# A transformer block pair on one core: own lane orders for PE, VectorE and ScalarE in the attention stage, gate rows by transposes, z products in column strips

## What is computed

```python
def first_block(x, c, ...):
    mod = (silu(c) @ w_ada + b_ada)
    h = rms_norm(x, g_pre_mix) * (1 + sc_m) + sh_m
    proj = h @ w_in                      # 2544 columns
    # group a: 8 heads, compressed + selected + window keys, gated sum
    # group b: 8 heads over a latent; an indexer keeps the 64 best of 256 keys per query:
    score = einsum('bths,bth->bts', relu(logits), wi_b)
    _, idx = top_k(score, 64)            # s // 4
    y = concat([o_a, o_b]) @ w_out
    x = x + ga_m * rms_norm(y, g_post_mix)
    x = x + ga_f * rms_norm(swiglu(...), g_post_ffn)

def second_block(x, c, ctx, ...):        # one layer, last: only the context's states are needed
    gq, gk, gv, gz, gg, rq, rk, rv, rg = split(h @ w_in)
    pre = gz.reshape(B, T, 2, 16) @ gla_gate_w + gla_gate_b    # gz is the "z" of the change
    ...
    x = x + mod[2] * x_out
    x = x + mod[5] * expert_choice_ffn(h2, ...)
    return rmsnorm(x, final_norm_w)
```

## Time and profile before

| what | value |
|---|---|
| time of the runs, median | 1354.22 us (1354.01 to 1354.99, 3 runs) |
| span of the profiled execution, first to last instruction | 1351.0 us |
| what the runs have beyond that span | 3.2 us (no other time is given for the profiled execution) |
| busy: PE, PEld, DVE, ACT, POOL | 1004.6, 582.0, 523.5, 292.5, 29.0 us |
| mean granted clock of PE | 0.869 |
| read from HBM | 413.26 MB, 307 GB/s over the span |

### The profile page before, as it was taken

One profiled execution on the slowest core, in us unless ns is written; L12 is line 12 of the kernel. 1 busy time (PEld: TensorE's weight loads), 2 busy tenths in 40 slices (PEclk: granted clock), 3 DMA queues, 4 the chain that ended last, 5 costly groups with the idle time before them and its releaser, 6 DMA issues.

```text
span 1351.0 us, 13067 instructions
## 1 busy us (share of the span) xinstructions
PE 1004.6 (74%) x5454; PEld 582.0 (43%) x5454; DVE 523.5 (39%) x995; ACT 292.5 (22%) x467; POOL 29.0 (2%) x38
## 2 busy tenths in 40 slices
PE   0796888899989999899997766555465555566585
PEld 0585667777666787687873211111111111111131
DVE  6876577687544498578663100000000000000001
ACT  2322344452242333562341100000000000000000
POOL 0001000000000000100110000000000000000000
PEclk9797798899989999899997867788867778766888
DMA  9796221567634469233269999999999999999996
GB/s 387 319 382 246 96 76 63 193 257 277 249 122 158 156 232 357 94 125 125 94 270 431 427 430 430 432 429 430 431 432 429 432 427 433 430 431 431 428 432 270
DMA packets 41147, 415.16 MB, mean 307 GB/s; under 512 B 4928, under 2 KB 4928, under 8 KB 7808
## 3 DMA queue, kind: packets, MB, share of 16 engines
q1 hardware_dynamic: 38304, 405.75, 73.2%
q10 hardware_dynamic: 2784, 8.57, 1.8%
HBM read 413.26 MB, written 1.05 MB: 307 GB/s over the span
## 4 chain that ended last, share of the span: by engine, by line
PE 43%; DMA 42%; DVE 10%; ACT 3%; issue 1%; POOL 0%; DVEq 0%; SPq 0%
DMA ring<-in_w_egu 25%; DMA ring<-in_w_ed 13%; PE PS L658 8%; PE PS L660 8%; PE PS L659 8%; PE PS L959 4%; PE PS L1275 3%; DMA arena<-in_w_ed 2%; PE PS L567 2%; DVE ringR L1496 2%; DMA ring<-in_w_in 1%; PE PS L1337 1%; DVE arena L1368 1%; ACT ringR L2403 1%; DVE ring L1410 1%
## 5 line engine op out<-in xcount | busy, mean ns | idle before, releaser
L1275 PE MATMUL PS<-ring,arena 128*32 128x512 f32 (+1 forms) x1152 | 173.1, 736 | 108.5 <-DMA ring<-in_w_egu 108.4
L658 PE MATMUL PS<-ringR,arenaR 128*128 128x512 f32 (+1 forms) x520 | 213.5, 411 | 21.5 <-DVE arenaR L1479 19.9
L660 PE MATMUL PS<-ringR,arenaR 128*128 128x512 f32 (+1 forms) x520 | 206.8, 398 | 0.0
L659 PE MATMUL PS<-ringR,arenaR 128*128 128x512 f32 (+1 forms) x520 | 206.6, 397 | 0.0
L1496 DVE TENSOR_TENSOR ringR<-ring,ringR 128x2048 fp32r<-128x2048 f32 (+1 forms) x66 | 148.7, 2254 | 98.1 <-ACT ringR L2403 98.0
L1368 DVE SCALAR_TENSOR_TENSOR arena<-arena,PS 128x256 f32<-128x256 f32 (+2 forms) x68 | 33.2, 497 | 370.5 <-ACT arena L2840 363.3
L2403 ACT ACTIVATE ringR<-ring 128x2048 fp32r<-128x2048 f32 (+1 forms) x66 | 123.9, 1885 | 89.2 <-PE PS L660 56.7
L1275 PEld LDWEIGHTS PS<-ring,arena 128*32 128x32 f32 x1152 | 36.3, 129 | 236.1 <-DMA ring<-in_w_egu 174.9
L1337 PE MATMUL PS<-ring,arena 128*32 128x512 f32 x512 | 88.3, 826 | 55.5 <-DMA ring<-in_w_ed 54.9
L658 PEld LDWEIGHTS PS<-ringR,arenaR 128*128 128x128 f32 x520 | 99.1, 191 | 48.1 <-DVE arenaR L1479 20.5
L2840 ACT ACTIVATE arena<-PS 128x512 f32<-128x512 f32 (+1 forms) x12 | 6.7, 561 | 502.6 <-PE PS L1275 502.6
(11 more groups left out here) (343 smaller groups left out, 878.1 us busy)
## 6 DMA issues: line engine op xcount, KB each, us to landing
ring<-in_w_egu SPq DMA_DIRECT2D x48, 2048.0 KB, 35.7
ring<-in_w_ed SPq DMA_DIRECT2D x32, 2048.0 KB, 33.8
ring<-in_w_vad SPq DMA_DIRECT2D x40, 1024.0 KB, 6.9
ring<-in_w_egu SPq DMA_DIRECT2D x24, 1536.0 KB, 29.6
arena<-in_w_egu SPq DMA_DIRECT2D x16, 2048.0 KB, 35.5
ring<-in_w_in SPq DMA_DIRECT2D x22, 1024.0 KB, 4.9
ring<-in_w_gu SPq DMA_DIRECT2D x22, 1024.0 KB, 4.8
arena<-in_w_ed SPq DMA_DIRECT2D x11, 2048.0 KB, 32.4
```

The costliest lines, as they stand in the source:

```text
L658: mm(o, xh(k, t), hi[:, c], start=k == 0, stop=False)
L659: mm(o, xh(k, t), s.viewr[:, c], start=False, stop=False)
L660: i = mm(o, xl(k, t), hi[:, c], start=False, stop=k == nk - 1)
L1275: i = mm(PS[32 * ee:32 * ee + 32, b + a_, 0:fw], XEv[:, k, grp, 32 * ee:32 * ee + 32], wv[:, ee, a_, :], start=k == 0, stop=k == 7, tile_p ...
```

## The change

Three orders of the lanes stand in the place of `ATT`: `ATT_PE` (102 letters), `ATT_DVE` (107) and `ATT_ACT` (93). Steps that do nothing at the end of a lane are left out. `sync` still makes its list of loads from `ATT`, so loads are issued in the same order as before. `gate_rows` uses the transpose helper `tr` instead of a matmul with the identity. The z products go into four strips of 32 output partitions, matmul k into strip k mod 4, two matmuls deep in each; the sum over the strips is left to the gate product, whose weights (`gate_w`) are stored four times, so it now contracts over 128 rows instead of 32, DVE copies 128 partitions instead of 32, and the load of `gate_w` is 256 KB instead of 64 KB.

```diff
 ATT, FFN = schedules()
+ATT_PE = ("p p f f p i c 1 i i 0 f c f 1 0 d d c 0 1 f d f c 1 i i 0 i i f c d 1 c f f c 1 0 f 1 d i i i i i i 0 f c c 1 d c i i 0 1 c f 1 0 f 0 d 0 1 f 1 f c c 0 1 c 0 i i 0 1 f i i 1 o o o 0 1 0 o o 0 o o 1 0 1 0").split()
+ATT_DVE = ("p p p f f c 1 0 d f f i c d c 1 1 0 0 f f d i i i c 1 c 0 f f c d i i o 1 1 c f f 1 d c 0 0 c i i i d c 0 1 1 f f c i 1 0 0 d i i 0 f f c 1 1 c i i 1 c 0 0 i i 0 f f i i 1 1 o o 0 0 i i i i i i 1 0 o o o o 1 1 0 0").split()
...
@@ gate_rows
-                    i = mm(PS[:, bank + c // 4, 128 * (c % 4):128 * (c % 4) + 128], gcol[:, 8 * q + c:8 * q + c + 1].broadcast_to([128, 128]), ident, start=True, stop=True)
+                    i = tr(PS[:, bank + c // 4, 128 * (c % 4):128 * (c % 4) + 128], gcol[:, 8 * q + c:8 * q + c + 1].broadcast_to([128, 128]))
@@ tensor
-            for k in ATT:
+            for k in ATT_PE:
                 next(lanes[k])
@@ context (and the same in w_in2 with bank 6, hT2)
                 for k in range(8):
-                    i = mm(PS[0:32, 7, 0:256], GZW[:, k, :], hcv[:, k, :], start=k == 0, stop=k == 7)
+                    j = k % 4
+                    i = mm(PS[32 * j:32 * j + 32, 7, 0:256], GZW[:, k, :], hcv[:, k, :], start=k < 4, stop=k >= 4, tile_position=(0, 32 * j))
...
-                    mm(PS[:, 7 - t, :], GZc[0:32, 128 * t:128 * t + 128], GWc[0:32, :], start=True, stop=True).then_inc(*sig("pe ctx pre", t))
+                    mm(PS[:, 7 - t, :], GZc[:, 128 * t:128 * t + 128], GWc, start=True, stop=True).then_inc(*sig("pe ctx pre", t))
...
-    d["gate_w"] = gw
+    d["gate_w"] = np.tile(gw, (4, 1))
```

More of the change, by code:

```diff
@@ L87 @@
 ATT, FFN = schedules()
+ATT_PE = ("p p f f p i c 1 i i 0 f c f 1 0 d d c 0 1 f d f c 1 i i 0 i i f c d 1 c f f c 1 0 f 1 d i i i i i i 0 f c c 1 d c i i 0 1 c f 1 0 f 0 d 0 1 f 1 f c c 0 1 c 0 i i 0 1 f i i 1 o o o 0 1 0 o o 0 o o 1 0 1 0").split()
+ATT_DVE = ("p p p f f c 1 0 d f f i c d c 1 1 0 0 f f d i i i c 1 c 0 f f c d i i o 1 1 c f f 1 d c 0 0 c i i i d c 0 1 1 f f c i 1 0 0 d i i 0 f f c 1 1 c i i 1 c 0 0 i i 0 f f i i 1 1 o o 0 0 i i i i i i 1 0 o o o o 1 1 0 0").split()
+ATT_ACT = ("p p f p i f f 1 0 1 c c 0 d d f f i i c c i i 1 1 f f o 1 0 0 f f o 0 c c c i i 1 1 f f 1 i i i i i i 0 0 c c c c 0 f f 1 1 d d d d d 1 0 0 f f 0 i i 1 1 i i 1 0 0 o o 0 i i 1 1 0 0 1 0").split()
 MIX_PE = ("w g w g w g w g g w g g w r g w g w w g g r w g r w g r w g g r w r g g g r w r r r").split()
@@ L1052, in w_in2 @@
                         for k in range(8):
-                            i = mm(PS[0:32, 6, 0:256], GZW[:, k, :], hT2[:, 256 * k:256 * k + 256], start=k == 0, stop=k == 7)
+                            j = k % 4
+                            i = mm(PS[32 * j:32 * j + 32, 6, 0:256], GZW[:, k, :], hT2[:, 256 * k:256 * k + 256], start=k < 4, stop=k >= 4, tile_position=(0, 32 * j))
                         i.then_inc(*sig("pe in2 z"))
@@ L1063, in gla @@
                 for t in range(2):
-                    mm(PS[:, t, :], GZx[0:32, 128 * t:128 * t + 128], GW2[0:32, :], start=True, stop=True).then_inc(*sig("pe gla pre", t))
+                    mm(PS[:, t, :], GZx[:, 128 * t:128 * t + 128], GW2, start=True, stop=True).then_inc(*sig("pe gla pre", t))
                 yield
@@ L1861, in vector @@
             lanes = {"p": prepare(), "f": adas(24, 32), "0": attention(0), "1": attention(1), "i": indexer(), "d": prepare_d(), "c": compress(), "o": out1()}
-            for k in ATT:
+            for k in ATT_DVE:
                 next(lanes[k])
@@ L1942, in context @@
                 w.wait_ge(*at("pe ctx z"))
-                cp(GZc[0:32, :], PS[0:32, 7, 0:256]).then_inc(*sig("v ctx z"))
+                cp(GZc, PS[:, 7, 0:256]).then_inc(*sig("v ctx z"))
                 yield
@@ L2026, in w_in2 @@
                         w.wait_ge(*at("pe in2 z"))
-                        cp(GZx[0:32, :], PS[0:32, 6, 0:256]).then_inc(*sig("v in2 z"))
+                        cp(GZx, PS[:, 6, 0:256]).then_inc(*sig("v in2 z"))
                     yield
@@ L2561, in scalar @@
             lanes = {"p": prepare(), "f": adas(24, 32), "0": attention(0), "1": attention(1), "i": indexer(), "d": prepare_d(), "c": compress(), "o": out1()}
-            for k in ATT:
+            for k in ATT_ACT:
                 next(lanes[k])
@@ L2611, in context @@
                 load("ctx", CXv, D["ctx"].rearrange("(t p) d -> p t d", p=128))
-                load("gw", GWc[0:32, :], D["gate_w"])
+                load("gw", GWc, D["gate_w"])
                 load("gateb", GBrc, row("gateb"))
@@ L2671, in scalar @@
             post("dn", 1, s22, th, lambda g, t: 2 - 2 * g + t)
-            load("gw2", GW2[0:32, :], D["gate_w"])
+            load("gw2", GW2, D["gate_w"])
             load("gateb2", GBr2, row("gateb"))
```

## The result

The changed kernel takes 1338.7 us in the median (4 runs, 1336.21 to 1348.86) where the kernel before, run beside it, takes 1354.12 (4 runs): a ratio of 0.9899, 95% interval 0.9865 to 0.9933. It is 15.4 us faster. The time lies inside the range of 1317 to 1345; the forecast of 1331.0 was 7.7 us too low.

A forecast was written before the change was run, and what follows sets the result against it. The expert weight stream sets the end; ahead of it the attention stage is bound by in-order engines waiting on one another. Terms 16.6 + 2.7 + 2.5 + 1.4 = 23.2 us, 1351.0 - 23.2 + 3.2 = 1331.0; range 1317 to 1345.

The forecast's parts named there:

- The stream: Expert weights from 688.78 us: length unchanged by the change, so whatever comes earlier before it moves the end equally.
- The start: Attention stage: PE begins its transposes at 103.9 us in place of 107.7, without waiting for DVE's last preparation: 3.8 us.
- The middle: Attention stage: three PE waits on DVE of 4.5, 3.4 and 2.9 us go away, 10.8 us.
- The tail: Attention stage's end: second top-k now right before the t = 1 pass, costing 4.7 us of new PE idle time.
- The clock: Attention stage: PE's loss to the lower clock level falls with idle time, from 18.7 to 12 us.
- Gate rows, z products: Gate rows by transposes gain 2.7 us; z products in strips gain 2.5 in the context lane and 1.4 in the mixer.
- C: Gate rows: transposing a broadcast column is dearer, each row 0.3 us slower, 2.7 turns to -0.9, 1334.6 us; chance 0.02.
- D: z products: the strips do not run side by side, 3.9 us less gain, 1334.9 us; chance 0.03.
- A: Attention stage: new order fits nearly as laid end to end, gain 33.6 in all, 1320.6 us; chance 0.22 with a little beyond.
- E: Attention stage: PE falls to low clock repeatedly from finer pieces, mean clock 0.60, 1384 us; chance 0.05 with other losses.
- B: Attention stage: stalls only move, idle and clock loss stay near 39 us, gain 3.8 to 8, 1340 to 1344; chance 0.18.
- F: Attention stage: something outside PE, DVE and ACT sets it, so the orders change nothing, 1347.6 us; chance 0.05.

The follow-up runs named there:

- e5: The changed kernel run again with no edit, on the same chip as three other runs: 1339.9 us, ratio 0.9884 to the kernel before.
- e8: The changed kernel with line 845's products widened from 30 to 128 columns and line 774's from 64 to 128: 1323.34 us, ratio 0.9765.
- e2: The kernel before with only gate rows by transposes and z products in strips, the old lane order kept on all engines: 1348.03 us, ratio 0.9936.
- e10: The three new lane orders alone, gate rows and z products as before, with lines 845 and 774 both 128 columns wide: 1328.22 us, ratio 0.9798.
- e1: The three new lane orders alone, gate rows by matmuls and z products in one strip as in the kernel before: 1343.25 us, ratio 0.9893.
- e9: The kernel before with line 842's and line 771's products widened to 128 columns (were 30 and 64): 1350.58 us, ratio 0.9972.
- e6: The kernel before with only line 842's products widened from 30 to 128 columns: 1348.87 us, ratio 0.9976.
- e7: The changed kernel with line 845's products widened from 30 to 64 columns: 1327.31 us, ratio 0.9808.
- e3: The changed kernel with line 845's products widened from 30 to 128 columns: 1330.75 us, ratio 0.9805.

## Why the forecast was 8 us off, step by step

**The stream.** Right: the issue of the first expert weights moved by 14.45 us and the span by 14.8.

**The start.** 3.8 forecast, 4.1 measured (107.74 to 103.65). Right; the new wait of 2.0 us behind it was not in the prediction.

**The middle.** 10.8 us of waits counted as gone; 4.5, 2.9 and 2.6 of the 3.4 are, together 10.0.

**The tail.** 4.7 us of new idle time forecast (its own terms, 4.1 and 12.3 less 11, add up to 5.4); the waits are 2.7 for the exponentials and 1.2 for the copies, 3.9. The second top-k stands where the prediction put it and takes 9.2 us where some 9 were estimated. Idle in all 10.5 where 13.5 was forecast. The first dsa maximum was to come 25 to 35 us before 214.50; on DVE it stands at 197.09 for the one head group and 201.78 for the other, 17.4 and 12.7 us earlier. That is the clock again: with the same orders the first stands at 189.47 in e5, 25.0 us earlier, and at 181.11 in e8, 33.4 us earlier.

**The clock.** This is the step that failed: "With idle time 13.5 in place of 19.6 us I scale the loss: ... I take 12." It measured 23.7 us in the profiled execution, 11.7 too much, and 15.6 in e5. The loss does not scale with idle time, since a part of it follows narrow products done without a wait. That the stage ended only 6.4 us late is luck: idle time and work came out 3.0 and 2.1 us smaller than forecast. The kernel before showed the second kind already at 144 us, on rows that I did not look at: the ada product behind line 842's products took 1.93 us at 145.42, right behind busy time. I read the earlier trace rows, where the low level came after a wait, and took it for the whole.

**Gate rows, z products.** 6.6 us in sum forecast, 5.8 by e2's issue and 5.9 by e8 against e10. In after's own trace, the context's strips give 2.57 us (forecast 2.5) and the mixer's 1.4 as forecast, with PE waiting 1.72 us for DVE's copy behind the remainder that was named. The copy of 128 partitions takes 0.42 us where that of 32 took 0.41, and the gate product over 128 rows 1.96 where it took 1.95: costed at nothing, rightly. The first gate row gives nothing: PE then waits 0.8 us for DVE's left operand (line 1484). Between the mixer's gate product and its gate row 1.57 us are lost again (16.97 us, 545.43 to 562.40, where it took 15.40), to a wait for ACT and not to the clock: the low level there costs about 1.6 us in both kernels, but PE waits 2.24 us for ACT where it waited 0.45, and ACT is busy 4.97 of 5 us. The first product behind that wait, of before and of after:

```profile
570.30 0.50 PE L658 MATMUL PS<-ringR,arenaR 128*128 128x512 f32 x1 [0.45 <-ACT arena L2697]
```

```profile
555.18 0.50 PE L661 MATMUL PS<-ringR,arenaR 128*128 128x512 f32 x1 [2.24 <-ACT arena L2702]
```

So my expectation for e2 gave the clock a loss that was ACT's.

**The rivals.** C and D are excluded by the 1.03 and 1.07 us. One transpose lasts 0.272 us in the profile, much as in C, but the eight overlap, so that eight times the length of one was the wrong sum. (A's 85% for DVE should have been 82, 92 of 112 us; nothing hangs on it.) E named the place, but not the cause: the low level did come for 27 us, from narrow products and not from waits, and the stage's clock of 0.80 stayed above the 0.73 at which it would have decided. B's time was close in after's profiled execution, for another reason: the stalls did not move, they went. A's stage end of 215.9 is near e8's 217.9, so with the clock held up the orders mesh almost as well as laid end to end. F is out, since the stage ended 10.0 us earlier and e1 gained 12.1. ACT shows no wait for a `w_out` load in the stage.

## What to carry to other kernels

Price a lower clock by what PE did before it fell, at each place where the trace shows it, not by scaling with idle time: here blocks of float32 products with 30 columns, and of 64 behind others with 16, had the low level behind them while PE looked full. Try to widen such products with data that is thrown away: here 128 columns cost next to no time, took 17 us off the changed kernel (1339.9 to 1323.34) and cut the scatter of its runs from 16 us to 2. A reordering that removes waits should be tried again after that: the orders alone gained 12.1 us with narrow products in both kernels and 22.4 us with wide ones, and the whole change 15 and 27. On the kernel before the same widening took only 4 to 5 us off (e9, e6), and it keeps a clock loss of 15.6 of 18.4 us.

## What was not expected of the hardware

A float32 product with 128 rows and 128 output partitions takes the same time, within 3%, for 30, 64 and 128 columns at the full level: line 845's 32 rows take 3.76 us (e5), 3.75 (e7) and 3.84 (e3). One program, twice profiled, had the same 27 us window at a granted clock of 0.50 and of 0.81 with the same 25.53 us of busy time. Why the chip lowers the clock behind narrow products was not shown. The profile models the ends of matmuls, so a string of narrow products that it counts as busy may still leave the array partly unused, and the runs do not tell the two apart. They show that the width alone, with the order kept, changes the granted clock of this stretch.
